# Hidden-state differences of product m6 made by VectorE instead of GpSimd, and residual reloads placed later in the load queue

## The chip, the cores and the metric

One NeuronCore of a Trainium2 chip. The metric is the device time of one launch in microseconds, the median of three runs. TensorE is called PE, VectorE DVE, ScalarE ACT, GpSimd POOL, and SyncE, whose queue issues all loads here, SP.

## The reference

A one-layer encoder trunk on 1024 tokens (two groups of 512) with width 1024. Attention and a recurrent mixer come first; the part that matters here is the second half of the layer:

```python
x = x + rmsnorm(mix, norm_mix_post[i])
h = rmsnorm(x, norm_mlp_pre[i])
m = jnp.square(jax.nn.relu(h @ w_up[i])) @ w_down[i]     # (1024 x 1024) @ (1024 x 4096), then (1024 x 4096) @ (4096 x 1024)
x = x + rmsnorm(m, norm_mlp_post[i])
e = p[i] @ w_ple[i]
gate = jax.nn.sigmoid(x @ w_ple_gate[i])
x = x + rmsnorm(e * gate, norm_ple[i])
```

All data are float32.

## The kernel before

**The work around the change.** The product with `w_down` is done by Strassen's scheme: instead of eight products of half-sized blocks there are seven, m1 to m7, each of a sum or difference of blocks of the hidden state (the operand) with a sum, difference or plain block of `w_down` (the weight). They are executed in the order of the list `products`: m4, m7, m1, m3, m5, m2, m6. Each product has 16 steps k over the contraction; a step is called a tile below, so the stage has 112 tiles. A tile is 12 matmuls of 128x512: four groups of 128 token rows, with three passes each (high x high, low x high, high x low), because every float32 number is split into a rounded high part and a rest.

**What each tile needs.** ACT makes the high parts (`wy_high` of the weight, L1392; `op_high` of the operand, L1423). POOL makes the low part of the weight, `wy_low` (L1449), and for every second tile of m7, m1 and m6 the weight's sum (`w_sum`, L1459). DVE makes the low part of the operand, `op_low` (L2194), the operand's sum where there is one (`op_sum`, L2187), the remaining weight sums (`w_sum`, L2171), and adds finished products to the result (`add_out`, L2212). All of them work up to two or three tiles ahead of PE: there are three buffers each for `wy_high`/`wy_low` (PAIRS) and for `op_high`/`op_low` (APAIRS). In the program's loops `low(pool, n + 2)`, `operand_sum(n + 3)`, `operand_low(n + 2)` stand for what is made while PE does tile n.

**The operand of m6** is the difference hid21 - hid11, one 128x512 tile for each k. These 16 differences are made ahead of m6, in place, by `hidden_difference`: eight during m5, six during m2 (four of them k = 10 to 13, then k = 0 and 1), and two (k = 14, 15) at the first tiles of m6. The table `difference_after` says behind which tile each is made. Before the change POOL makes them (L1478), right after the `wy_low` of that tile; since POOL runs two tiles ahead, the one behind tile n falls into PE's tile n - 2.

**The operand of m2** is a sum that was kept in DRAM (`keep_e`) for its first 14 tiles; SP loads it back tile by tile, beside the weight, in a ring of six buffers.

**Between m2 and m6.** When m5 is done, the first half of the result is complete. During m2, ACT squares it (`squares8`), DVE makes the mean (`means8`, behind tile 6), POOL the reciprocal root (`roots_of`, L2044, at its tile 7), and DVE does `add8(t)` for t = 0 to 3 behind tiles 8, 10, 12, 14 of m2: a 128x1024 product with the gain (L2223) and the addition to the residual `x_res` (L2227). For that the residual must be back from DRAM: SP reloads it (`x_res<-keep_x`, L1872, 512 KB for each t), t = 0 to 3 behind loads of m2, and t = 4 to 7, which `add8` needs only after m6, behind loads of m6. The first of each four waits for an addition that frees the space: that of m5 (`add_out("m5", 3, "12")`), which DVE does at tile 3 of m2, and that of m2 (`add_out("m2", 3, "22")`) at tile 7 of m6. The addition of t = 0 waits for all four reloads of its half. PE transposes the new residual at tiles 5, 8, 10 and 12 of m6 (L1566).

Each engine works off its own instructions in the order written; the engines wait for each other by counters.

Of the kernel before, what the change touches and what calls it, by code (L numbers as in the profile page):

```python
# [54 lines left out]
def trunk_kernel(nc, x, p, norm_mix_pre, w_in, w_uq, w_ukv, att_out_norm, hg_lb, hg_out_norm,  # L55
                 w_o, norm_mix_post, norm_mlp_pre, w_up, w_down, norm_mlp_post, w_ple, w_ple_gate, norm_ple,
                 rope_cos, rope_sin, latent_gain, y):
    with ExitStack() as top:
# [983 lines left out]
        def back_of():  # L1042
# [6 lines left out]
            minus = ("m4", "m3")  # L1049
            segs = [("wo", 0, h, n) for h in range(2) for n in range(2)]  # L1050
# [57 lines left out]
            def pool_sums(n):  # L1108

                if n >= TILES:  # L1110
                    return False
                (kind, _, _, _), k = segs[tiles_of[n][0]], tiles_of[n][1]
                if kind == "st":
                    return st_order[k] in ("t2", "t4")
                return kind == "m" and products[segs[tiles_of[n][0]][1]] in ("m7", "m1", "m6") and k % 2 == 1
# [4 lines left out]
            raws, splits = [], []  # L1120
            for n in range(TILES):
# [12 lines left out]
                splits.append(("pair", n))  # L1134
                if n in difference_after:
                    splits.append(("difference", difference_after[n]))
                for r in res_after.get(n, []):
                    raws.append(("res", r))
                    splits.append(("res", r))
            raw_at = {tile: q for q, tile in enumerate(raws)}  # L1140
            place = {tile: q for q, tile in enumerate(splits)}
            high_at = {tile: q for q, tile in enumerate(tile for tile in splits if tile[0] in ("pair", "res"))}
# [4 lines left out]
            a_sum_at = {n: i for i, n in enumerate(a_sums)}  # L1147
# [144 lines left out]
            def score_slices(part):  # L1292

                kind, one, two = part
                if kind == "q":
# [29 lines left out]
             hid21_in, hid_summed, sums_kept, w_sum_made, op_sum_made, op_high_made, op_low_made, out_act, out_dve) = (  # L1325
                 sem(top, "st_" + n) for n in (
                     "x_moved", "s_step", "s_split", "s_high", "t_made", "p1_made", "first_added", "first", "u", "comb", "late", "hid11_in",
                     "hid21_in", "hid_summed", "sums_kept", "w_sum", "op_sum", "op_high", "op_low", "out_act", "out_dve"))
# [29 lines left out]
            def sum_tile(n):  # L1358

                s, k = tiles_of[n]  # L1360
                return t_sum[int(st_order[k][1])][:, :] if segs[s][0] == "st" else w_sum[(n - M_TILE) % 2]

# [44 lines left out]
            def op_high_of(act, n):  # L1407
# [5 lines left out]
                elif name == "m6":  # L1413
                    act.wait_ge(low_made, place["difference", k] + 1)
                elif name == "m2" and k < SUMMED:
                    raw_ready(act, ("e", n))
                else:
                    act.wait_ge(op_sum_made, a_sum_at[n] + 1)
# [32 lines left out]
            def weight_sum(pool, n):  # L1451
                s, k = tiles_of[n]
                if segs[s][0] == "m":
# [3 lines left out]
                    if sum_before(n) is not None:  # L1457
                        pool.wait_ge(low_made, place["pair", sum_before(n)] + 1)
# [14 lines left out]
            def hidden_difference(pool, k):  # L1473
                pool.wait_ge(hid11_in, 16 * len(SPILLS))
                pool.wait_ge(hid21_in, 16 * BLOCKS)
                if k >= SUMMED:
                    pool.wait_ge(op_sum_made, a_sum_at[first[M2] + k] + 1)
                pool.tensor_tensor(hid21[k], hid21[k], hid11[k], ALU.subtract).then_inc(low_made, 1)  # L1478

            def low(pool, n):  # L1480
                if n < TILES:
                    if pool_sums(n + 1):
                        weight_sum(pool, n + 1)
                    low_part(pool, ("pair", n))
                    if n in difference_after:
                        hidden_difference(pool, difference_after[n])
# [283 lines left out]
            def sp_tail(sp):  # L1770
# [9 lines left out]
                def freed(raw):  # L1780
                    name, n = raw
                    if name in ("pair", "res"):
# [9 lines left out]
                    elif raw_of(("pair", n)) is not None:  # L1792
                        sp.wait_ge(low_made, place["pair", n] + 1)
# [28 lines left out]
                back_after = {m_raw("m2", 7 + i): i for i in range(4)}  # L1822
                back_after.update({m_raw("m6", 11 + i): 4 + i for i in range(4)})
                for q in range(len(raws)):
# [26 lines left out]
                    if q in hid11_after:  # L1851
                        b = hid11_after[q]
                        if b == SPILLS[0]:
                            sp.wait_ge(late_made, 6 * BLOCKS)
                            sp.wait_ge(low_made, place["pair", M_TILE - 1] + 1)
# [17 lines left out]
                    if q == m_raw("m2", 2):  # L1873
                        sp.wait_ge(low_made, place["difference", 3] + 1)
                        sp.wait_ge(op_sum_made, a_sum_at[first[M5] + 15] + 1)
# [189 lines left out]
            def dve_tail(dve):  # L2065
# [92 lines left out]
                def down_weight_sum(n):  # L2158
# [10 lines left out]
                    elif sum_before(n) is not None:  # L2169
                        dve.wait_ge(low_made, place["pair", sum_before(n)] + 1)  # L2170
# [3 lines left out]
                def operand_sum(n):  # L2174
                    if n not in a_sum_at:
# [444 lines left out]
```

## Time and profile before

| | |
|---|---|
| median of 3 runs | 1431.26 us (1430.6 to 1433.81) |
| profiled execution, its own time | 1430.18 us |
| its span | 1428.6 us |
| mean granted PE clock | 0.994 |
| PE busy | 1388.5 us, 97% of the span |
| PE weight loads busy | 1146.0 us, 80% |
| DVE busy | 912.4 us, 64% |
| POOL busy | 810.8 us, 57% |
| ACT busy | 659.4 us, 46% |

A busy time counts an instruction from its start to its end, and also what it waits in between for a port. The span is that from the first to the last instruction; the time of the execution has 1.6 us around it.

### The profile page before, as it was taken

The page shows a single profiled execution, that of the slowest core. Times are in us where ns is not written, and L with a number is a line of the kernel's source. Part 1 is how long each engine was busy: PE and PEld are TensorE (multiplying, and loading weights), DVE is VectorE, ACT ScalarE, POOL GpSimd, SP SyncE. Part 2 cuts the span into 40 slices and gives each one's busy share as a digit, 9 for nine tenths or more (in the row PEclk, how much of TensorE's full clock was granted, in tenths as well). Part 3 has the DMA queues.
Part 4 walks back from the last instruction along what each step waited for, and adds up shares of the span by engine and source line. Part 5 has one row for each costly group of instructions (what it writes and reads, how often), then busy time and mean ns, then how long its engine had stood idle before and what let it go on. Part 6 is the DMA issues. An engine that isn't in the chain of part 4 may idle for free.

```text
span 1428.6 us, 19101 instructions
## 1 busy us (share of the span) xinstructions
PE 1388.5 (97%) x6868; PEld 1146.0 (80%) x6868; DVE 912.4 (64%) x1096; ACT 659.4 (46%) x1225; POOL 810.8 (57%) x612
## 2 busy tenths in 40 slices
PE   7999999999999999999999999999999999889998
PEld 5888888878848999887888888888766878768876
DVE  6135555436587877165665556558999898785375
ACT  6223222324337765355765554545443444335452
POOL 4374636356306433455577777765777477765481
PEclk9999999999999999999999999999999999999999
DMA  6221011102240003434543443438466724655252
GB/s 206 67 67 38 23 39 29 31 26 60 67 102 2 1 1 104 170 104 140 185 125 104 125 125 97 132 109 296 163 198 212 252 89 151 218 164 176 89 165 86
DMA packets 138253, 162.08 MB, mean 113 GB/s; under 512 B 16688, under 2 KB 82224, under 8 KB 138160
## 3 DMA queue, kind: packets, MB, share of 16 engines
q1 hardware_dynamic: 138160, 160.87, 35.7%
q8 instruction: 55, 0.90, 0.2%
q14 instruction: 38, 0.31, 0.1%
HBM read 139.86 MB, written 18.87 MB: 111 GB/s over the span
## 4 chain that ended last, share of the span: by engine, by line
PE 80%; DVE 12%; issue 3%; POOL 2%; DMA 1%; ACT 1%; SPq 0%; DVEq 0%; POOLq 0%; ACTq 0%
PE ps L50 21%; PE ps L52 21%; PE ps L51 21%; DVE op_low L2194 4%; PE ps L921 4%; PE ps L1757 4%; DVE op_sum L2187 3%; DVE w_sum L2171 2%; PE ps L1764 2%; PE ps L1566 1%; PE ps L1014 1%; POOL wy_low L1449 1%; PE ps L968 1%; PE ps L953 1%; DMA w_raw<-keep_e 1%
## 5 line engine op out<-in xcount | busy, mean ns | idle before, releaser
L1449 POOL TENSOR_TENSOR wy_low<-w_raw,wy_high 128x512 fp32r<-128x512 f32 x118 | 176.2, 1495 | 120.7 <-ACT wy_high L1392 120.5
L50 PE MATMUL ps<-wy_high,op_high 128*128 128x512 f32 x448 | 180.0, 402 | 15.3 <-DVE op_low L2194 15.1
L51 PE MATMUL ps<-wy_low,op_high 128*128 128x512 f32 x448 | 176.1, 393 | 0.0
L52 PE MATMUL ps<-wy_high,op_low 128*128 128x512 f32 x448 | 176.1, 393 | 0.0
L1449 POOL TENSOR_TENSOR wy_low<-w_sum,wy_high 128x512 fp32r<-128x512 f32 x80 | 121.3, 1523 | 76.0 <-ACT wy_high L1392 75.9
L369 POOL TENSOR_TENSOR wx_low<-w_raw,wx_high 128x512 fp32r<-128x512 f32 (+1 forms) x64 | 84.2, 1321 | 140.4 <-ACT wx_high L471 140.4
L1392 ACT ACTIVATE wy_high<-w_raw 128x512 fp32r<-128x512 f32 x118 | 74.3, 630 | 153.6 <-PE ps L52 147.5
L50 PEld LDWEIGHTS ps<-wy_high,op_high 128*128 128x128 f32 x448 | 85.2, 190 | 45.4 <-POOL wy_low L1449 16.3
L1449 POOL TENSOR_TENSOR wy_low<-t_sum,wy_high 128x512 fp32r<-128x512 f32 x64 | 89.5, 1398 | 53.8 <-ACT wy_high L1392 53.8
L1392 ACT ACTIVATE wy_high<-w_sum 128x512 fp32r<-128x512 f32 x80 | 50.6, 632 | 126.0 <-PE ps L52 67.5
L50 PE MATMUL ps<-h_high,wx_high 128*128 128x512 f32 (+1 forms) x256 | 102.6, 401 | 0.0
L50 PE MATMUL ps<-a_high,wy_high 128*128 128x512 f32 x256 | 100.1, 391 | 0.8 <-DVE hid L2111 0.8
L52 PEld LDWEIGHTS ps<-wy_high,op_low 128*128 128x128 f32 x448 | 85.1, 190 | 18.4
L52 PE MATMUL ps<-h_high,wx_low 128*128 128x512 f32 (+1 forms) x256 | 99.8, 390 | 0.0
L51 PE MATMUL ps<-h_low,wx_high 128*128 128x512 f32 (+1 forms) x256 | 99.8, 390 | 0.0
L52 PE MATMUL ps<-a_high,wy_low 128*128 128x512 f32 x256 | 99.6, 389 | 0.0
L51 PE MATMUL ps<-a_low,wy_high 128*128 128x512 f32 x256 | 99.6, 389 | 0.0
L51 PEld LDWEIGHTS ps<-wy_low,op_high 128*128 128x128 f32 x448 | 85.3, 190 | 16.5
L515 ACT ACTIVATE k_pick<-kk 128x512 f32<-128x512 f32 x56 | 35.9, 669 | 114.3 <-DVE kk L688 108.0
L50 PE MATMUL ps<-wy_high,a_high 128*128 128x512 f32 x224 | 88.6, 396 | 0.0
L685 DVE TENSOR_TENSOR qq<-qq,totals 128x512 f32<-128x512 f32 x48 | 41.3, 861 | 72.3 <-PE ps L921 72.3
L52 PE MATMUL ps<-wy_high,a_low 128*128 128x512 f32 x224 | 87.4, 390 | 0.0
(270 smaller groups left out, 3658.8 us busy)
## 6 DMA issues: line engine op xcount, KB each, us to landing
w_raw<-in_w_down SPq DMA_DIRECT2D x127, 256.0 KB, 3.4
raw_more<-in_w_down SPq DMA_DIRECT2D x65, 256.0 KB, 3.4
w_raw<-in_w_up SPq DMA_DIRECT2D x64, 256.0 KB, 3.3
w_raw<-in_w_in SPq DMA_DIRECT2D x62, 256.0 KB, 2.8
w_raw<-in_w_o SPq DMA_DIRECT2D x32, 256.0 KB, 2.6
raw_more<-in_w_up SPq DMA_DIRECT2D x32, 256.0 KB, 3.3
w_raw<-in_w_ple_gate SPq DMA_DIRECT2D x32, 256.0 KB, 2.6
keep_h<-comb SPq DMA_DIRECT2D x26, 256.0 KB, 2.3
```

Of the source, the lines that this page charges most:

```text
L50: pe.matmul(out, stat_high, mov_high, start=start, stop=False)
L51: pe.matmul(out, stat_high, mov_low, start=False, stop=False)
L52: return pe.matmul(out, stat_low, mov_high, start=False, stop=stop)
L369: pool.tensor_tensor(out, raw, high.bitcast(F32), ALU.subtract).then_inc(w_low_made, 1)
L515: act.activation(k_pick[:, g, l % 2, :].rearrange("p (b h t) -> p b h t", h=2, t=1 << l), halves(kk, g, l, False), ACT.Copy).then_inc(k_pi ...
L685: dve.tensor_tensor(queries, queries, factors(g, l, True), ALU.mult).then_inc(q_decayed, 1)
L921: last = pe.matmul(ps[:, 4 + g, ch * P:(ch + 1) * P], k_pick[:, g, l % 2, ch * P:(ch + 1) * P], halves(qq, g, l, True, ch, 1), start=True, ...
L1392: act.activation(out, tile_raw(tile), ACT.Copy).then_inc(high_made, 1)
L1449: pool.tensor_tensor(low_tile, tile_raw(tile), high_tile.bitcast(F32), ALU.subtract).then_inc(low_made, 1)
L1757: last = pe.matmul(ps[:, 4 + tr % 2, hr * VD:(hr + 1) * VD], prob_t[:, r % 2, k, :], v_att[:, tr // QT * QT + k, hr * VD:(hr + 1) * VD], s ...
L2187: dve.tensor_tensor(op_sum[n % 2], one[k], two[k], ALU.subtract if name == "m7" else ALU.add).then_inc(op_sum_made, 1)
L2194: dve.tensor_tensor(op_low[n % APAIRS][:, :], op_raw(n), op_high[n % APAIRS][:, :].bitcast(F32), ALU.subtract).then_inc(op_low_made, 1)
```

## The change

Three things change.

1. The differences go from POOL to DVE. `low` on POOL no longer makes them; DVE's loop calls `hidden_difference(difference_after[n])` at tile n, behind `operand_low(n + 2)`. The table stays the same, so each is also made two tiles later than before in PE's terms. They count on the counter of operand sums (`op_sum_made`), and whoever waited for them waits there.
2. The reloads of the residual for t = 0 to 3 stand behind the loads of tiles 9 to 12 of m2 instead of 7 to 10; those for t = 4 to 7 stand behind the last load of m6 and the three loads after it (of the gate product) instead of behind tiles 11 to 14 of m6.
3. Code that would let DVE make the low parts of some weights is added, with an empty list `low_on_dve`, so it issues nothing.

```diff
@@ the tables
+            low_on_dve = ()
...
-                splits.append(("pair", n))
-                if n in difference_after:
-                    splits.append(("difference", difference_after[n]))
+                highs.append(("pair", n))
+                if not low_by_dve(n):
+                    splits.append(("pair", n))
...
-            a_sum_at = {n: i for i, n in enumerate(a_sums)}
+            a_made = []
+            for n in range(M_TILE, M_TILE + MSTEPS + 3):
+                a_made += [("sum", n)] if n in a_sums else []
+                a_made += [("difference", difference_after[n - 3])] if n - 3 in difference_after else []
+            made_at = {made: i for i, made in enumerate(a_made)}
@@ ACT: op_high_of
                 elif name == "m6":
-                    act.wait_ge(low_made, place["difference", k] + 1)
+                    act.wait_ge(op_sum_made, made_at["difference", k] + 1)
@@ POOL
-            def hidden_difference(pool, k):
-                pool.wait_ge(hid11_in, 16 * len(SPILLS))
-                pool.wait_ge(hid21_in, 16 * BLOCKS)
-                if k >= SUMMED:
-                    pool.wait_ge(op_sum_made, a_sum_at[first[M2] + k] + 1)
-                pool.tensor_tensor(hid21[k], hid21[k], hid11[k], ALU.subtract).then_inc(low_made, 1)
...
-                    low_part(pool, ("pair", n))
-                    if n in difference_after:
-                        hidden_difference(pool, difference_after[n])
+                    if not low_by_dve(n):
+                        low_part(pool, ("pair", n))
@@ SP
-                back_after = {m_raw("m2", 7 + i): i for i in range(4)}
-                back_after.update({m_raw("m6", 11 + i): 4 + i for i in range(4)})
+                back_after = {m_raw("m2", 9 + i): i for i in range(4)}
+                back_after.update({m_raw("m6", 15) + i: 4 + i for i in range(4)})
...
                     if q == m_raw("m6", 7):
-                        sp.wait_ge(low_made, place["difference", BLOCKS - 1] + 1)
+                        sp.wait_ge(op_sum_made, len(a_made))
@@ DVE
+                def hidden_difference(k):
+                    if k == 2:
+                        dve.wait_ge(hid21_in, 16 * BLOCKS)
+                    if k >= SUMMED:
+                        dve.wait_ge(op_sum_made, made_at["sum", first[M2] + k] + 1)
+                    dve.tensor_tensor(hid21[k], hid21[k], hid11[k], ALU.subtract).then_inc(op_sum_made, 1)
...
                     down_weight_sum(n + 3)
                     operand_sum(n + 3)
                     operand_low(n + 2)
+                    weight_low(n + 2)
+                    if n in difference_after:
+                        hidden_difference(difference_after[n])
```

**DVE, from behind tile 7 of m2 to behind tile 11.** The first pair L2223, L2227 (before) or L2247, L2251 (after) is `add8(0)`. Before:

```order
L2194 TENSOR_TENSOR op_low0_219<-w_raw,op_high0_216 128x512
L2223 SCALAR_TENSOR_TENSOR total_116<-total_116,y_stat12_134,gain_mlp_244 128x1024
L2227 TENSOR_TENSOR x_res_119<-x_res_119,total_116 128x1024
L2194 TENSOR_TENSOR op_low1_220<-w_raw,op_high1_217 128x512
L2194 TENSOR_TENSOR op_low2_221<-raw_more1_159,op_high2_218 128x512
L2223 SCALAR_TENSOR_TENSOR total_116<-total_116,y_stat12_134,gain_mlp_244 128x1024
L2227 TENSOR_TENSOR x_res_119<-x_res_119,total_116 128x1024
L2187 TENSOR_TENSOR op_sum0_222<-hid21_14_214,p1_kept_160 128x512
L2194 TENSOR_TENSOR op_low0_219<-w_raw,op_high0_216 128x512
```

After:

```order
L2205 TENSOR_TENSOR op_low0_219<-w_raw,op_high0_216 128x512
L2247 SCALAR_TENSOR_TENSOR total_116<-total_116,y_stat12_134,gain_mlp_244 128x1024
L2251 TENSOR_TENSOR x_res_119<-x_res_119,total_116 128x1024
L2205 TENSOR_TENSOR op_low1_220<-w_raw,op_high1_217 128x512
L2219 TENSOR_TENSOR hid21_0_200<-hid21_0_200,hid11_0_166 128x512
L2205 TENSOR_TENSOR op_low2_221<-raw_more1_159,op_high2_218 128x512
L2247 SCALAR_TENSOR_TENSOR total_116<-total_116,y_stat12_134,gain_mlp_244 128x1024
L2251 TENSOR_TENSOR x_res_119<-x_res_119,total_116 128x1024
L2198 TENSOR_TENSOR op_sum0_222<-hid21_14_214,p1_kept_160 128x512
L2205 TENSOR_TENSOR op_low0_219<-w_raw,op_high0_216 128x512
L2219 TENSOR_TENSOR hid21_1_201<-hid21_1_201,hid11_1_167 128x512
```

Two subtractions into hid21, for k = 0 and k = 1, stand between the low parts and the additions.

**POOL at the same place**, around the reciprocal root of the first half (`y_stat12<-y_stat11`). Before:

```order
L1478 TENSOR_TENSOR hid21_13_213<-hid21_13_213,hid11_13_179 128x512
L1449 TENSOR_TENSOR wy_low_120<-w_raw,wy_high_121 128x512
L1449 TENSOR_TENSOR wy_low_120<-raw_more0_158,wy_high_121 128x512
L1478 TENSOR_TENSOR hid21_0_200<-hid21_0_200,hid11_0_166 128x512
L2044 TENSOR_TENSOR y_stat12_134<-y_stat11_133,minus_half 128x4
L1449 TENSOR_TENSOR wy_low_120<-w_raw,wy_high_121 128x512 x2
L1478 TENSOR_TENSOR hid21_1_201<-hid21_1_201,hid11_1_167 128x512
L1449 TENSOR_TENSOR wy_low_120<-raw_more0_158,wy_high_121 128x512
L1449 TENSOR_TENSOR wy_low_120<-w_raw,wy_high_121 128x512 x3
L1459 TENSOR_TENSOR w_sum1_225<-w_raw 128x512
```

After:

```order
L1466 TENSOR_TENSOR wy_low_120<-w_raw,wy_high_121 128x512 x2
L1466 TENSOR_TENSOR wy_low_120<-raw_more0_158,wy_high_121 128x512
L2055 TENSOR_TENSOR y_stat12_134<-y_stat11_133,minus_half 128x4
L1466 TENSOR_TENSOR wy_low_120<-w_raw,wy_high_121 128x512 x2
L1466 TENSOR_TENSOR wy_low_120<-raw_more0_158,wy_high_121 128x512
L1466 TENSOR_TENSOR wy_low_120<-w_raw,wy_high_121 128x512 x3
L1476 TENSOR_TENSOR w_sum1_225<-w_raw 128x512
```

The three differences of this piece (one further up, one right ahead of the root, one between the low parts behind it) are gone; the low parts of the weights and the weight's sum keep their order.

**SP's queue in m2**, from the load of tile 7's weight on. `w_raw` and `raw_more` are the ring of six buffers. Before:

```order
L1778 DMA w_raw<-in_w_down 128x512
L1872 DMA x_res_119<-keep_x 128x1024
L1778 DMA w_raw<-keep_e 128x512
L1778 DMA w_raw<-in_w_down 128x512
L1872 DMA x_res_119<-keep_x 128x1024
L1778 DMA w_raw<-keep_e 128x512
L1778 DMA raw_more0_158<-in_w_down 128x512
L1872 DMA x_res_119<-keep_x 128x1024
L1778 DMA raw_more1_159<-keep_e 128x512
L1778 DMA w_raw<-in_w_down 128x512
L1872 DMA x_res_119<-keep_x 128x1024
```

After:

```order
L1787 DMA w_raw<-in_w_down 128x512
L1787 DMA w_raw<-keep_e 128x512
L1787 DMA w_raw<-in_w_down 128x512
L1787 DMA w_raw<-keep_e 128x512
L1787 DMA raw_more0_158<-in_w_down 128x512
L1883 DMA x_res_119<-keep_x 128x1024
L1787 DMA raw_more1_159<-keep_e 128x512
L1787 DMA w_raw<-in_w_down 128x512
L1883 DMA x_res_119<-keep_x 128x1024
L1787 DMA w_raw<-keep_e 128x512
L1787 DMA w_raw<-in_w_down 128x512
L1883 DMA x_res_119<-keep_x 128x1024
L1787 DMA w_raw<-keep_e 128x512
L1787 DMA raw_more0_158<-in_w_down 128x512
L1883 DMA x_res_119<-keep_x 128x1024
```

Four loads of m2 (the kept operands of tiles 7 and 8, the weights of tiles 8 and 9) now stand ahead of the first reload.

## Rows read from the trace of the kernel before

**Rows 1.** PE busy by stretch: window in us, its length, busy us (matmuls), clock, DMA share, GB/s
```profile
1109.56:1153.08 43.52, 43.52 (x193) 1.00 0.66 208
1153.08:1198.22 45.14, 44.34 (x194) 1.00 0.34 109
1198.22:1248.21 49.99, 46.00 (x193) 0.97 0.61 205
1248.21:1305.49 57.28, 50.87 (x225) 0.94 0.58 195
```

**Rows 2.** timeline of PE: start us, duration us, what, [idle before it <-releaser]
```profile
1219.98 0.46 PE L50 MATMUL ps<-wy_high,op_high 128*128 128x512 f32 x1
...
1231.89 0.76 PE L50 MATMUL ps<-wy_high,op_high 128*128 128x512 f32 x1 [3.10 <-DVE op_low L2194]
...
1255.16 0.47 PE L50 MATMUL ps<-wy_high,op_high 128*128 128x512 f32 x1 [4.07 <-DVE op_low L2194]
...
1279.33 1.68 PE L1566 MATMUL ps<-ident,x_res 128*128 128x128 f32 x8 [2.35 <-DVE total L2212]
```

**Rows 3.** PE busy and clock in the stretches behind the first two waits
```profile
1231.80:1235.20 3.40, 3.31 (x8) 0.50 0.61 179
...
1255.10:1259.30 4.20, 4.14 (x11) 0.59 0.65 215
```

**Rows 4.** timeline of all engines in one tile of m3
```profile
1147.64 0.39 PE L50 MATMUL ps<-wy_high,op_high 128*128 128x512 f32 x1
1147.77 0.69 DVE L2187 TENSOR_TENSOR op_sum<-hid,hid 128x512 f32<-128x512 f32 x1
...
1148.61 1.30 POOL L1449 TENSOR_TENSOR wy_low<-w_raw,wy_high 128x512 fp32r<-128x512 f32 x1 [1.42 <-ACT wy_high L1392]
...
1149.09 1.37 DVE L2194 TENSOR_TENSOR op_low<-op_sum,op_high 128x512 fp32r<-128x512 f32 x1 [0.63 <-ACT op_high L1423]
```

**Rows 5.** timeline of DVE in m5
```profile
1168.36 1.67 DVE L2187 TENSOR_TENSOR op_sum<-hid,hid 128x512 f32<-128x512 f32 x1
1169.95 1.78 DVE L2194 TENSOR_TENSOR op_low<-op_sum,op_high 128x512 fp32r<-128x512 f32 x1
1171.76 1.67 DVE L2187 TENSOR_TENSOR op_sum<-hid,hid 128x512 f32<-128x512 f32 x1
```

**Rows 6.** timeline of POOL in m5
```profile
1169.44 1.74 POOL L1478 TENSOR_TENSOR hid<-hid,hid 128x512 f32<-128x512 f32 x1
```

**Rows 7.** timeline of DVE in the second half of m2
```profile
1224.41 1.20 DVE L2194 TENSOR_TENSOR op_low<-w_raw,op_high 128x512 fp32r<-128x512 f32 x1 [1.48 <-ACT op_high L1423]
1225.53 2.31 DVE L2223 SCALAR_TENSOR_TENSOR total<-total,y_stat,gain_mlp 128x1024 f32<-128x1024 f32 x1
1227.88 2.19 DVE L2227 TENSOR_TENSOR x_res<-x_res,total 128x1024 f32<-128x1024 f32 x1
1230.00 1.75 DVE L2194 TENSOR_TENSOR op_low<-w_raw,op_high 128x512 fp32r<-128x512 f32 x1
...
1233.34 1.27 DVE L2223 SCALAR_TENSOR_TENSOR total<-total,y_stat,gain_mlp 128x1024 f32<-128x1024 f32 x1
1234.65 1.22 DVE L2227 TENSOR_TENSOR x_res<-x_res,total 128x1024 f32<-128x1024 f32 x1
```

**Rows 8.** timeline of POOL there
```profile
1222.33 1.46 POOL L2044 TENSOR_TENSOR y_stat<-y_stat,minus_half 128x4 f32<-128x4 f32 x1
...
1226.73 2.26 POOL L1478 TENSOR_TENSOR hid<-hid,hid 128x512 f32<-128x512 f32 x1
```

**Rows 9.** waits of SP's queue from 1195 to 1310 us: total us, times, longest
```profile
SPq L1872 <- DVE total L2212: 12.8, 2, 8.9
```

**Rows 10.** waits of ACT from 1210 to 1230 us: total us, times, longest
```profile
ACT op_high L1423 <- DMA w_raw<-keep_e: 2.9, 2, 1.6
...
ACT op_high L1423 <- DMA raw_more<-keep_e: 1.3, 1, 1.3
```

**Rows 11.** issues of the first and the fourth reload (1210.3 to 1210.7, 1214.6 to 1215): KB, us to landing
```profile
x_res<-keep_x SPq DMA_DIRECT2D x1, 512.0 KB, 3.6
...
x_res<-keep_x SPq DMA_DIRECT2D x1, 512.0 KB, 8.4
```

**Rows 12.** groups of instructions from 1153 to 1305 us: count, busy us, mean ns, idle before
```profile
L2212 DVE TENSOR_TENSOR total<-part,ps 128x512 f32<-128x512 f32 x16 | 10.5, 674 | 0.0
```

More of the change, by code:

```diff
@@ L1114, in pool_sums, with low_by_dve @@
                     return st_order[k] in ("t2", "t4")
-                return kind == "m" and products[segs[tiles_of[n][0]][1]] in ("m7", "m1", "m6") and k % 2 == 1
+                return kind == "m" and products[segs[tiles_of[n][0]][1]] in ("m7", "m1", "m6") and k % 2 == 1 and not low_by_dve(n)
+            def low_by_dve(n):
+                return in_m(n) and m_step(n)[0] in low_on_dve
             difference_after = {first[M5] + 2 * i + 1: 2 + i for i in range(8)}
@@ L1139, in back_of @@
                     splits.append(("res", r))
+                    highs.append(("res", r))
             raw_at = {tile: q for q, tile in enumerate(raws)}
             place = {tile: q for q, tile in enumerate(splits)}
-            high_at = {tile: q for q, tile in enumerate(tile for tile in splits if tile[0] in ("pair", "res"))}
+            high_at = {tile: q for q, tile in enumerate(highs)}
+            low_at = {n: i for i, n in enumerate(n for n in range(TILES) if low_by_dve(n))}
             w_sums = [n for n in range(M_TILE, M_TILE + MSTEPS) if len(quads[m_step(n)[0]]) == 2 and not pool_sums(n)]
@@ L1361, in sum_tile, with low_ready @@
                 return t_sum[int(st_order[k][1])][:, :] if segs[s][0] == "st" else w_sum[(n - M_TILE) % 2]
+            def low_ready(engine, n):
+                if low_by_dve(n):
+                    engine.wait_ge(w_low_made, low_at[n] + 1)
+                else:
+                    engine.wait_ge(low_made, place["pair", n] + 1)
             def sum_before(n):
@@ L1457, in weight_sum @@
                     if sum_before(n) is not None:
-                        pool.wait_ge(low_made, place["pair", sum_before(n)] + 1)
+                        low_ready(pool, sum_before(n))
                     pool.tensor_tensor(sum_tile(n), raw_tile(one), raw_tile(two),
@@ L1792, in freed @@
                     elif raw_of(("pair", n)) is not None:
-                        sp.wait_ge(low_made, place["pair", n] + 1)
+                        low_ready(sp, n)
                     else:
@@ L1854, in sp_tail @@
                             sp.wait_ge(late_made, 6 * BLOCKS)
-                            sp.wait_ge(low_made, place["pair", M_TILE - 1] + 1)
+                            low_ready(sp, M_TILE - 1)
                             for i in range(4):
@@ L2169, in down_weight_sum @@
                     elif sum_before(n) is not None:
-                        dve.wait_ge(low_made, place["pair", sum_before(n)] + 1)
+                        low_ready(dve, sum_before(n))
                     dve.tensor_tensor(sum_tile(n), raw_tile(one), raw_tile(two),
@@ L2524, in pe_tail @@
                     n, last_k, width = first[a] + b, depth[segs[a][0]] - 1, len(banks_of(a))
-                    pe.wait_ge(low_made, place["pair", n] + 1)
+                    low_ready(pe, n)
                     wh, wl = wy_high[:, n % PAIRS, :], wy_low[:, n % PAIRS, :]
```

23 lines of the change are left out of this document (15 added, 8 removed).

## The prediction

> **What bounds the kernel now.** I read first how long PE takes for each product, from the view of busy time by stretch [rows 1]. m3 takes 43.52 us for 16 tiles without a gap: 2.72 us a tile, PE's own pace. m5 takes 45.14 us, 1.6 more. m2 takes 49.99, 6.5 more. m6 takes 57.28, of which four transposes of eight matmuls each are work (about 0.8 us each, 3.3 together), so it loses some 10.5. Only these losses can be won: the products before m5 hold nothing that the change touches, and behind m6 only the place of the reloads differs.
>
> Next, where PE stands, from its timeline [rows 2]. It waits 3.10 us for the low operand of tile 11 of m2 (until 1231.89), 4.07 us for that of tile 1 of m6 (until 1255.16), and 2.35 us at the second transpose of m6 for an addition by DVE. Behind each wait the clock is at the lower of its two levels, 1.2 GHz, for about 3.4 us [rows 3]: 3.40 us at 0.50, so about 1.7 us of PE's work is lost on top of the wait. I call T8 the start of tile 8 of m2, 1219.98 [rows 2]; from there to 1255.16, where tile 1 of m6 starts, nine tiles take 35.2 us instead of 24.5.
>
> So DVE is late in m2. Why, the timelines of DVE and POOL tell. Where they don't meet, DVE needs 0.69 us for a 128x512 tile from two SBUF operands, and POOL 1.30 [rows 4]. The DVE instruction that starts while POOL's runs takes 1.37, and ends 0.55 us after POOL's end (1149.91 to 1150.46). In m5 POOL makes differences too [rows 6], the two alternate, and each DVE instruction takes 1.67 to 1.78, starts 1.6 to 1.8 apart [rows 5]: 0.6 of work and 1.1 behind one of POOL's. An addition that reads PSUM takes 0.67 on the mean over the same stretch [rows 12] and seems never to wait. So count turns: a DVE instruction 0.6, a POOL instruction that gets ahead of it 1.1.
>
> **Differences in m5 (eight).** Now a pair of tiles in m5 has on DVE 2 operand sums and 2 low parts (4 x 0.6), on POOL 3 instructions (3 x 1.1): 5.7 us of turns in 5.44 us of PE. That is over PE's pace, and the rows show tiles of 3.4 us, DVE-bound. After: 5 x 0.6 + 2 x 1.1 = 5.2 us, below it. The additions of m3 in tiles 0 to 3 (0.6 each, no turn) lie beside POOL's turns. In the steady tile of m3, POOL starts 0.97 us after the tile's start and DVE's low part ends 2.82 us after it (1147.64 to 1150.46) [rows 4]; it is needed two tiles on, at 5.44, so 2.6 us are spare, more than a difference costs even in its worst turn (1.75). I take **-1.6 us** for m5, all its loss. Bounds: 0 if every DVE instruction still meets POOL, -1.6 at best.
>
> The Trainium skill speaks against this step (the page SBUF — State Buffer, section "SBUF: two separate sides"): the port pair that VectorE and GpSimd share is an exclusive lock, held for the whole instruction, and the loser stands still. The rows agree that the loser stands still. With the whole 1.30 us of POOL's instruction as its turn, a pair of tiles would hold 2 x 1.3 + 5 x 0.6 = 5.6 us, over 5.44, and m5 would lose 8 x 0.16 = 1.3 us as it does now, so the step would bring 0.3 instead of 1.6.
>
> **Reloads in m2.** The first reload waits for DVE's addition at tile 3. SP stands there 12.8 - 8.9 = 3.9 us [rows 9], and behind it the kept operands and weights of tiles 7 to 9. Then four times 512 KB go out among them, and ACT waits 2.9 + 1.3 us for kept operands [rows 10]. The low part of tile 10 thus starts at 1224.41, ends at 1225.6, and `add8(0)` follows [rows 7]. After the change the first reload is queued behind tile 9's weight, which itself needs a buffer that tile 6's low weight frees; by then the addition of tile 3 is done, so SP doesn't stand, and a tile of 2.72 us carries 1 MB. The operands come in time. The low part of tile 10 is then done at the steady place, T8 + 2.8 (1222.8), 2.8 us earlier. The root, at 1222.33 to 1223.79 now [rows 8], moves up too: its input no longer waits for late operands and no difference is ahead of it.
>
> The reload of t = 3 goes out with tile 12's weight, about T8 - 0.2. Landing took 3.6 us for the first and 8.4 for the fourth of the present burst [rows 11]; spread out, I take 5, so T8 + 4.8, and the addition of `add8(0)` wants it at T8 + 5.2. Tight; late by 3 us at the upper bound.
>
> **m2 from tile 8 on.** Here the count goes along DVE's order, with 0.6 for a 512-wide instruction, 1.3 and 1.2 for the two halves of `add8` (the last two of [rows 7]), and 1.1 for each POOL instruction that has become ready. In us behind T8: low part of tile 10 done 2.8; `add8(0)` first half 4.1; POOL 5.2; second half 6.4; low part of tile 11 **7.0** (PE wants it at 8.2: the 3.10 us wait is gone); POOL and difference 0 until 8.7; low part of tile 12 9.3 (wanted 10.9); POOL, half, half of `add8(1)` 13.0; POOL, operand sum 14.7; POOL 15.8; low part of tile 13 **16.4**, wanted at 13.6. So a wait comes back two tiles later: 2.8 us, and the clock falls, 1.7. Then difference 1 17.0, sum and low part of tile 14 18.2, `add8(2)` 20.7, POOL's weight sum 21.8, weight sum and low part of tile 15 23.0 (in time), low part of m6 tile 0 24.8, `add8(3)` with two POOL turns 29.5, weight sum and low part of m6 tile 1 **30.7**, wanted at 29.0. PE starts that tile at 30.8 instead of 35.2: **-4.4 us**. The differences 0 and 1 cost 1.2 us in this chain; what they replace is POOL's four differences in it (0, 1, 14, 15), of which each stood before a DVE instruction: 2.19, 2.31 and 1.75 us in a row [rows 7] for 1.2, 1.3 and 0.6. The second bound: if the freed turns bring nothing, the chain is only 2.8 us earlier and 1.2 longer, -1.6. At best the wait at tile 13 doesn't come, and -9 stands.
>
> The wait ahead of m6 tile 1 shrinks from 4.07 to about 1.8 us. The clock fell behind waits of 2.35 and more [rows 2, 3]; in m5, which loses 1.6 us in short waits, it stays at 1.00 [rows 1]. I take it that it stays up: **-1.7 us**; 0 is the other bound.
>
> **Start of m6.** Differences 14 and 15 are now DVE's, at tiles 0 and 1, beside additions, low parts and a weight sum: 1.2 us in a place where DVE is behind, at worst 2 x 1.75 = 3.5. Whatever is not made up until tile 7 lengthens PE's wait for the last addition there (2.35 us [rows 2]), since DVE comes to it in order. I take **+1.2 us**.
>
> **Reloads in m6.** SP stands 8.9 us [rows 9] before the reload of t = 4 and holds the loads of tiles 12 and 13 back. PE doesn't wait for these: m6's loss of 10.5 is used up by its two waits [rows 2] and 1.7 of clock behind each, so tiles 8 to 15 are at pace. After, they come early and the reloads go with the gate's first weights, 2 MB and 1 MB, wanted after m6. 0, covered by m6's last four tiles (11 us); uncovered, it would show as a wait of gate tile 1 or 2. The load of `gain_ple`, which waited for POOL's difference 15, now waits for DVE's, some 1 to 3 us, with two weights behind it that are wanted a tile or two later: 0.
>
> **Sum.** -1.6 - 4.4 - 1.7 + 1.2 = -6.5 us against the profiled execution: 1430.18 - 6.5 = 1423.7, span about 1422.1. That execution is 1.1 below the median, so the median to expect is 1431.26 - 6.5 = **1424.8**.
>
> **Rivals.** (a) *No wait comes back at tile 13.* POOL and DVE fall in step so that DVE meets fewer of its instructions. For it: in one row pair `add8(1)` runs free (1.27, 1.22). Against: it ran free because PE stood and POOL had no work. Gain 1.6 + 9 + 0 to 1.7: about 1420. Chance 0.15. (b) *Half the gain:* the clock falls ahead of m6 as well and DVE's backlog is carried to the second transpose in full, +2.7 instead of +1.2: -1.6 - 4.4 + 2.7 = -3.3, 1428. For it: DVE's gaps in m6 between tiles 1 and 7 are small. Chance 0.2. (c) *The reloads are late.* All four must have landed for `add8(0)`; with 8.4 us they land 3 us late, the low part of tile 11 at T8 + 10: -3.5, 1427.8. It decides above 5 us of landing. Chance 0.1. (d) *Slower:* the four differences on the late DVE cost a full turn each, 4 x 1.75 = 7.0, because POOL, ahead with less to do, is always ready when DVE ends; only m5's 1.6 and the 2.8 of the operands stand against it: +2.6, 1433.9. It decides when POOL meets more than two of three DVE instructions from T8 on. Against: POOL has 4 instructions fewer there. Chance 0.07. (e) *Nothing:* DVE's total of work is longer by 16 x 0.6 us and the gain in m5 and m2 is given back in m6, so only a shift of the waits is left: 1431, 0.06. My forecast has the rest, 0.42.
>
> **Numbers.** A run of this kernel can be told from no change beyond about 0.2%, 2.9 us: below 1428.4 is faster. My own case (1422 to 1427) and (a) count wholly as faster, (b) and (c) by about two thirds: 0.42 + 0.15 + 0.2 = 0.77. Slower is (d), 0.07. The rest, 0.16, is the same. The range leaves out half of (a) below and (d) and part of (e) above: 1419.5 to 1430.5.
>
> **What the changed profile would show.** m5 at 43.5 us; no L2219 longer than 1.8; no wait of SP's reload for DVE and no wait of ACT for `keep_e`; tile 11 of m2 without a wait, one of 2 to 3 us at tile 13 with half clock behind it; m6 tile 1 at most 2 us late and at full clock; the wait at m6's second transpose at 2 to 5 us. Wrong would be: the second half of `add8(0)` waiting for a DMA, or DVE's instructions behind tile 8 as long as now.

## The result, and the profile after

| | before | changed |
|---|---|---|
| median of the runs timed together | 1432.53 us (6 runs, 1430.6 to 1434.12) | 1424.24 us (6 runs, 1422.3 to 1427.27) |
| profiled execution: its time, span | 1430.18, 1428.6 us | 1422.3, 1420.5 us |
| mean granted PE clock | 0.994 | 0.997 |
| DVE busy, POOL busy | 912.4, 810.8 us | 907.0, 780.1 us |

The ratio is 0.9945, 95% interval 0.9929 to 0.9961: 8 us faster, with 5.6 to 10 in the interval. The forecast was 6.5.

Busy time of PE by stretch, m3, m5, m2, m6 as in [rows 1], and then the rest of the span, in the changed kernel:

```profile
1110.28:1153.80 43.52, 43.52 (x194) 1.00 0.66 207
1153.80:1197.32 43.52, 43.52 (x194) 1.00 0.37 114
1197.32:1245.43 48.11, 44.49 (x193) 1.00 0.63 211
1245.43:1298.68 53.25, 48.10 (x225) 1.00 0.63 210
1298.68:1420.50 121.82, 114.67 (x529) 0.98 0.34 110
```

m5 is at PE's own pace, m2 is 1.9 us shorter and m6 4.0. (Behind m6 it is 121.8 us instead of 123.1; m5 starts 0.7 us later.) The clock is 1.00 from m3 to m6; before the change it fell in m2 (0.97) and m6 (0.94). That is not wholly the change's doing, as a second profile of the same kernel showed (below, `changed_again`).

PE's timeline, as in [rows 2], with T8 first and then every wait up to tile 1 of m6:

```profile
1219.08 0.39 PE L50 MATMUL ps<-wy_high,op_high 128*128 128x512 f32 x1
...
1227.97 0.47 PE L50 MATMUL ps<-wy_high,op_high 128*128 128x512 f32 x1 [0.57 <-DVE op_low L2205]
1235.02 0.47 PE L50 MATMUL ps<-wy_high,op_high 128*128 128x512 f32 x1 [1.36 <-DVE op_low L2205]
1242.63 0.47 PE L50 MATMUL ps<-wy_high,op_high 128*128 128x512 f32 x1 [1.69 <-DVE op_low L2205]
1250.26 0.47 PE L50 MATMUL ps<-wy_high,op_high 128*128 128x512 f32 x1 [1.95 <-DVE op_low L2205]
```

In place of waits of 3.10, 0.77 and 4.07 us, at tiles 11 and 15 of m2 and tile 1 of m6, there are four of 0.57 to 1.95 us, at tiles 11, 13 and 15 of m2 and tile 1 of m6. From T8 to the last of them it is 31.2 us instead of 35.2. SP's queue no longer waits for DVE's additions [rows 9]; its new wait, that of the load of `gain_ple` for difference 15, is short:

```profile
SPq L1891 <- DVE hid L2219: 0.3, 1, 0.3
```

ACT waits for no kept operand [rows 10]. But DVE now waits for the reload, 1.82 us ahead of the second half of `add8(0)`; the prediction had named this wait as a sign of being wrong (timeline of DVE, which answers to [rows 7]):

```profile
1220.52 1.36 DVE L2205 TENSOR_TENSOR op_low<-w_raw,op_high 128x512 fp32r<-128x512 f32 x1 [0.76 <-ACT op_high L1440]
1221.80 1.27 DVE L2247 SCALAR_TENSOR_TENSOR total<-total,y_stat,gain_mlp 128x1024 f32<-128x1024 f32 x1
1224.90 1.23 DVE L2251 TENSOR_TENSOR x_res<-x_res,total 128x1024 f32<-128x1024 f32 x1 [1.82 <-DMA x_res<-keep_x]
1226.04 1.78 DVE L2205 TENSOR_TENSOR op_low<-w_raw,op_high 128x512 fp32r<-128x512 f32 x1
1227.74 0.68 DVE L2219 TENSOR_TENSOR hid<-hid,hid 128x512 f32<-128x512 f32 x1
```

The fourth reload was issued at 1219.02, 0.06 us ahead of T8, and took longer to land than the 5 us that I had taken (issues from 1219.0 to 1219.4):

```profile
x_res<-keep_x SPq DMA_DIRECT2D x1, 512.0 KB, 5.8
```

### The profile page after: what moved, and what is told of

Same layout as the page of the kernel before. It is cut to its first block, busy times and chain, and to the rows that moved or that the text cites. A ratio compares the mean times of both kernels' runs of the same rounds, so it can differ in the third digit from the quotient of the medians.

```text
span 1420.5 us, 19085 instructions
## 1 busy us (share of the span) xinstructions
PE 1381.4 (97%) x6868; PEld 1141.4 (80%) x6868; DVE 907.0 (64%) x1112; ACT 657.6 (46%) x1225; POOL 780.1 (55%) x596
## 4 chain that ended last, share of the span: by engine, by line
PE 82%; DVE 11%; issue 3%; DMA 1%; POOL 1%; ACT 1%; SPq 0%; DVEq 0%; POOLq 0%; ACTq 0%
PE ps L50 22%; PE ps L52 22%; PE ps L51 22%; PE ps L921 4%; PE ps L1766 4%; DVE op_low L2205 3%; DVE op_sum L2198 2%; DVE w_sum L2182 2%; PE ps L1773 2%; PE ps L1575 1%; PE ps L1014 1%; PE ps L968 1%; PE ps L953 1%; PE ps L965 1%; DMA k_t<-k_rope 0%
## 5 line engine op out<-in xcount | busy, mean ns | idle before, releaser
L51 PE MATMUL ps<-wy_low,a_high 128*128 128x512 f32 x224 | 87.2, 389 | 0.0
```

The lines of the kernel that those rows point to most:

```text
L51: pe.matmul(out, stat_high, mov_low, start=False, stop=False)
```

## The experiments

All were timed in five rounds beside the kernel before. Ratios are to that kernel. Where I compare with the changed kernel, I use the lengths of the stages in the profiles (one profiled execution for each run), which repeat to 0.1 us where nothing is late, while single runs of one kernel lie up to 7 us apart.

### Each half of the change alone

`differences_alone`: the reloads back.

```diff
-                back_after = {m_raw("m2", 9 + i): i for i in range(4)}
-                back_after.update({m_raw("m6", 15) + i: 4 + i for i in range(4)})
+                back_after = {m_raw("m2", 7 + i): i for i in range(4)}
+                back_after.update({m_raw("m6", 11 + i): 4 + i for i in range(4)})
```

> The changed kernel with both groups of reloads at their old places, so the differences are DVE's and nothing else differs from before. Theory A (each part has its own share: fewer port turns for DVE, and operands that come in time): m5 falls from 45.1 to 43.5 us; in m2 SP still stands about 4 us before the first reload and ACT still waits about 4 us for kept operands, so add8(0) starts as late as before, but with fewer turns behind it; in all 3 to 5 us faster than before, ratio 0.997. Theory B (the reloads' place does it, the differences win only in m5): 1.6 us faster, 0.999, and tile 11 of m2 waits 3 us as before. Theory C (the differences do it all): 8 us faster, 0.9945.

`reloads_alone`: the kernel before with the two new lines.

> The kernel before with both groups of reloads at their new places; the differences stay on POOL. Theory A: m5 stays at 45.1 us; kept operands come in time, the low part of tile 10 is done 2 to 3 us earlier, but POOL's difference stands ahead of the root and the turns of POOL stay, so m2 and m6 together lose 2 to 3 us less: 2 to 3 us faster, ratio 0.998. Theory B: 6 us faster, 0.996. Theory C: no change, 1.000.

Both medians are 1429.03 us, both ratios 0.997 (0.9959 to 0.9982, and 0.9957 to 0.9983). Each half gives 0.3%, together they give 0.55%: theory A. B and C fall by `differences_alone`, whose interval holds neither the 0.999 of B nor the 0.9945 of C; `reloads_alone` alone would not tell A (0.998) from B (0.996), but it excludes C (1.000). The stages m5, m2, m6 of `differences_alone`:

```profile
1157.24:1200.76 43.52, 43.52 (x193) 1.00 0.36 115
1200.76:1251.90 51.14, 44.73 (x193) 1.00 0.59 199
1251.90:1307.05 55.15, 50.84 (x225) 0.94 0.59 202
```

and of `reloads_alone`:

```profile
1154.17:1199.30 45.13, 44.36 (x193) 1.00 0.34 109
1199.30:1247.20 47.90, 44.33 (x194) 1.00 0.63 212
1247.20:1305.64 58.44, 52.03 (x226) 0.91 0.56 192
```

The differences win m5 (43.52) and the start of m6; with the old reloads m2 is even longer than before (51.14 against 49.99), with waits at tiles 8, 11, 13 and 15. The reloads' place wins m2 (47.90), but m6 still waits 4.07 us for its tile 1, as before, and at a clock of 0.91 instead of 0.94 takes 1.2 us longer. In `differences_alone` SP stands before its reloads, and ACT waits even longer than before for kept operands (waits of SP from 1195 to 1310 us, of ACT from 1195 to 1250):

```profile
SPq L1883 <- DVE total L2236: 12.5, 2, 7.8
...
ACT op_high L1440 <- DMA w_raw<-keep_e: 6.4, 3, 2.6
```

### Where the gain in m5 comes from

`m5_on_pool`: differences 2 to 9 back on POOL, the others on DVE.

```diff
+            on_pool = tuple(range(2, 10))
...
+                    if difference_after.get(n) in on_pool:
+                        k = difference_after[n]
+                        pool.wait_ge(hid11_in, 16 * len(SPILLS))
+                        pool.wait_ge(hid21_in, 16 * BLOCKS)
+                        pool.tensor_tensor(hid21[k], hid21[k], hid11[k], ALU.subtract).then_inc(low_made, 1)
...
-                    if n in difference_after:
+                    if n in difference_after and difference_after[n] not in on_pool:
                         hidden_difference(difference_after[n])
```

> The changed kernel with the eight differences of m5 back on POOL; the other eight stay on DVE. Theory A (turns: 5.7 us a pair of tiles against 5.2): m5 is back at 45.1 us with low parts and sums of 1.7 us, m2 and m6 as in the changed kernel (48.1 and 53.2 us): 1.6 us slower than the changed kernel. Rival (the lock is held for POOL's whole instruction, so m5 is bound either way, or the m5 gain came from elsewhere): m5 stays within 0.3 us of 43.5.

`all_in_m5`: fourteen differences behind tiles 1 to 14 of m5.

```diff
-            difference_after = {first[M5] + 2 * i + 1: 2 + i for i in range(8)}
-            difference_after.update({first[M2] + 2 * i + 1: (10 + i) if i < 4 else i - 4 for i in range(6)})
+            difference_after = {first[M5] + 1 + i: (2 + i) if i < 12 else i - 12 for i in range(14)}
```

> The changed kernel with the fourteen differences 2 to 13, 0 and 1 behind tiles 1 to 14 of m5, one each, none in m2. Theory A (turns: 6 x 0.6 + 2 x 1.1 = 5.8 us for a pair of tiles against PE's 5.44): m5 becomes DVE-bound in its second half, 45 to 46 us instead of 43.5; m2 has two differences fewer where DVE is late, 1.2 us less: in all 0 to 1.5 us slower than the changed kernel. Rival 1 (turns cost DVE more, a full 1.7 for each instruction): m5 over 50 us. Rival 2 (a difference costs DVE only its 0.6 where POOL is idle, 4 x 0.6 + 2 x 0.6 + 1.3 = 4.9 a pair): m5 stays at 43.5 us.

`m5_on_pool`: 1425.15 us, ratio 0.9947 (0.9931 to 0.9963). `all_in_m5`: 1424.83 us, 0.9944 (0.993 to 0.9957). In time neither is told apart from the changed kernel; in m5 they are (busy time of PE in m5, first `m5_on_pool`):

```profile
1153.55:1198.66 45.11, 44.34 (x194) 1.00 0.34 109
```

and `all_in_m5`, m5 and m2:

```profile
1155.37:1200.06 44.69, 44.53 (x193) 1.00 0.36 110
1200.06:1246.10 46.04, 44.09 (x193) 1.00 0.66 222
```

With the differences back on POOL the 1.6 us are back. With one on DVE for every tile m5 is 1.2 us over PE's pace, where rival 2 wanted none and rival 1 a stage of over 50. I had written 45 to 46 us and got 44.69: tiles 0 to 8 take 2.72 us, since DVE enters the stage ahead, and only tiles 9 to 13 take 2.91 to 3.04. In those tiles the turns can be read one by one (timeline of DVE and POOL in `all_in_m5`):

```profile
1186.70 1.32 POOL L1465 TENSOR_TENSOR wy_low<-w_raw,wy_high 128x512 fp32r<-128x512 f32 x1 [1.59 <-ACT wy_high L1408]
1186.78 1.79 DVE L2204 TENSOR_TENSOR op_low<-op_sum,op_high 128x512 fp32r<-128x512 f32 x1
1188.49 0.68 DVE L2218 TENSOR_TENSOR hid<-hid,hid 128x512 f32<-128x512 f32 x1
1189.09 0.68 DVE L2197 TENSOR_TENSOR op_sum<-hid,hid 128x512 f32<-128x512 f32 x1
1189.69 1.78 DVE L2204 TENSOR_TENSOR op_low<-op_sum,op_high 128x512 fp32r<-128x512 f32 x1
```

DVE's instructions start 1.71, 0.60 and 0.60 us apart: 2.91 us a tile, 5.8 a pair, which is the count of 6 x 0.6 + 2 x 1.1. The one that meets POOL's ends 0.55 us behind POOL's end, as in [rows 4]. So the count tells whether DVE binds: at 5.7 and 5.8 us a pair m5 is longer than PE's 43.5 us, at 5.2 it isn't. It doesn't tell how long the stage becomes: 5.8 gave 44.69 and 5.7 gave 45.11. DVE's lead counts as well (tiles 0 to 8 at pace); what else makes this difference was not tested. The rule of the Trainium skill (the page SBUF — State Buffer, section "SBUF: two separate sides"), taken with the whole 1.3 us for POOL, asked for 1.3 us of loss in the changed m5. The profile has none; the measurement decides for 1.1. That the loser stands still is what all these rows show.

The groups of instructions from 1154 to 1197 us, a stretch that lies within m5 in both kernels, of `m5_on_pool`: mean ns of one ahead of the second bar:

```profile
L2217 DVE TENSOR_TENSOR op_low<-op_sum,op_high 128x512 fp32r<-128x512 f32 x14 | 20.3, 1453 | 0.1
L2210 DVE TENSOR_TENSOR op_sum<-hid,hid 128x512 f32<-128x512 f32 x13 | 18.1, 1391 | 0.3
```

and of the changed kernel:

```profile
L2205 DVE TENSOR_TENSOR op_low<-op_sum,op_high 128x512 fp32r<-128x512 f32 x14 | 17.9, 1281 | 1.9 <-ACT op_high L1440 1.8
L2198 DVE TENSOR_TENSOR op_sum<-hid,hid 128x512 f32<-128x512 f32 x13 | 13.3, 1022 | 0.2
L2219 DVE TENSOR_TENSOR hid<-hid,hid 128x512 f32<-128x512 f32 x7 | 4.7, 678 | 0.0
```

Without POOL's differences an operand sum takes 1.02 us on the mean instead of 1.39, a low part 1.28 instead of 1.45, and the differences themselves 0.68. DVE makes the eight differences as well, and yet its busy time in m5 falls, from 42.4 us in `m5_on_pool` to 39.3 in the changed kernel.

### What each difference costs where DVE is late

`early_0_1`: differences 0 and 1 behind tiles 4 and 6 of m2 instead of 9 and 11.

```diff
-            difference_after.update({first[M2] + 2 * i + 1: (10 + i) if i < 4 else i - 4 for i in range(6)})
+            difference_after.update({first[M2] + 2 * i + 1: 10 + i for i in range(4)})
+            difference_after.update({first[M2] + 4: 0, first[M2] + 6: 1})
```

> The changed kernel with the differences 0 and 1 made behind tiles 4 and 6 of m2, where DVE stands idle 1.3 us a tile, instead of behind 9 and 11. Theory A (each costs the late DVE 0.6 us, up to 1.7 with a turn): the chain up to m6 tile 1 is 1.2 us shorter, m2 and the first tiles of m6 together 1.2 us less; 1 us faster. Rival (the port turns bind, not DVE's own work): below 0.3 us.

1422.79 us, ratio 0.9925 (0.9911 to 0.9939): the lowest median here. m2 takes 46.01 us, 2.1 less than in the changed kernel's first profile and 1.65 less than in its second, against 1.2 expected. What is over 1.2 is not the two instructions' doing: the fourth reload landed after 4.4 us in this execution, and after 5.8 and 5.3 in those two. `m6_reloads_back` (below) has the m2 of the changed kernel and ends `add8(0)` 6.2 us behind T8, as this run does, and its m2 takes 47.22 us: 1.2 more, as expected. `all_in_m5` has the same 46.04 in m2, which shows it a second time.

`early_and_later` does this and moves differences 14 and 15 from behind tiles 0 and 1 of m6 to tiles 2 and 3.

```diff
-            difference_after.update({first[M6] + i: 14 + i for i in range(2)})
+            difference_after.update({first[M6] + 2 + i: 14 + i for i in range(2)})
```

> Differences 0 and 1 behind tiles 4 and 6 of m2, and 14 and 15 behind tiles 2 and 3 of m6 instead of 0 and 1. Theory A (each of them costs the late DVE 0.6 to 1.7 us at the start of m6): the waits at tiles 2 and 4 of m6 (0.3 and 0.8 us) shrink or move, since DVE catches up only towards tile 7: the same as with the early differences alone, up to 0.5 us, ratio 0.9925. Rival (they cost their full turn and nothing takes it back): 1 us faster.

1426.68 us, 0.9959 (0.9946 to 0.9971): both theories wrong, it is slower than `early_0_1`. m2 is the same (46.04), m6 56.73 us instead of 53.22. The waits tell why: of SP's queue from 1195 to 1310 us, of DVE and of PE from 1244 to 1300:

```profile
SPq L1892 <- DVE hid L2220: 7.1, 1, 7.1
...
DVE w_sum L2183 <- DMA w_raw<-in_w_down: 3.6, 1, 3.6
...
PE ps L1576 <- DVE total L2237: 5.4, 2, 4.3
```

The load of `gain_ple` overwrites operands of the differences, so it waits for the last of them, now 7.1 us. Behind it in the queue are weights of m6; DVE waits 3.6 us for one, and its additions, which stand behind that sum, hold up PE's second transpose for 4.3 us instead of 2.3. Behind that longer wait the clock falls, where in `early_0_1` it stays up: PE is busy 49.4 us in m6 instead of 48.1, so 1.3 of the 3.5 us are the clock's. Two tiles of delay of a 0.6 us instruction cost 3.5 us by way of the queue. I had named this wait in the prediction for the changed kernel and priced it at nothing, which was right there (0.3 us).

### The reloads' place, finer

`m2_reloads_8`: the changed kernel with `m_raw("m2", 8 + i)` instead of `9 + i`.

> The changed kernel with the first four reloads one tile earlier, behind the loads of tiles 8 to 11 of m2. Theory A (add8(0) waits 1.82 us for the fourth reload, and everything behind it is late by that): the wait goes, tile 11 starts without one, the chain of DVE up to m6 tile 1 ends 1 to 2 us earlier: 1 to 2 us faster than the changed kernel, unless the operands of tiles 9 and 10 come late. Rival (DVE's turns with POOL bind, the wait only lets POOL go first): the same up to 0.5 us, since the waits at tiles 13 and 15 take it back.

`early_and_8`: the same on top of `early_0_1`.

> Differences 0 and 1 behind tiles 4 and 6 of m2, and the first four reloads behind tiles 8 to 11. Theory A (the earlier reload meets DVE's addition again, SP stands 2 us and the kept operand of tile 8 comes late, which costs as much as the wait at add8(0)): m2 0 to 1 us longer than with the early differences alone (46.0 us). Rival (only the wait at add8(0) counts): m2 0.5 us shorter.

1425.54 us, 0.9944 (0.993 to 0.9957), and 1423.33 us, 0.9928 (0.9915 to 0.9941). The wait of `add8(0)` for the reload is gone in both, and nothing is won: m2 takes 48.58 us in the first (46.66 in the second, 0.65 longer than with the early differences alone). SP stands again 2.0 us for DVE's addition at tile 3, and ACT waits 4.2 us in all for kept operands (waits of SP, then of ACT, in `m2_reloads_8`):

```profile
SPq L1883 <- DVE total L2236: 2.0, 1, 2.0
...
ACT op_high L1440 <- DMA w_raw<-keep_e: 2.6, 2, 1.3
ACT op_high L1440 <- DMA raw_more<-keep_e: 1.6, 1, 1.6
```

So one tile earlier is too early: DVE doesn't wait at `add8(0)`, but comes to it later. The wait that the place of the change brings is 1.82 us in its first profile, with other lengths in others, since the same reload took 4.9 to 5.8 us to land. DVE gets some 1.0 us of it back: while it stands, POOL's instruction gets through, and the second half of `add8(0)` then takes 1.23 us, where it takes 2.21 in `m2_reloads_8`. What counts is when `add8(0)` is done:

| | DVE's wait for the reload | `add8(0)` done behind T8 | m2 |
|---|---|---|---|
| `m6_reloads_back` | 0.89 us | 6.2 us | 47.22 us |
| `changed_again` | 1.36 | 6.6 | 47.66 |
| `m5_on_pool` | 1.48 | 6.7 | 47.79 |
| changed kernel | 1.82 | 7.1 | 48.11 |
| `m2_reloads_8` | none | 7.4 | 48.58 |
| `early_0_1` | 0.48 | 6.2 | 46.01 |
| `early_and_8` | none | 6.8 | 46.66 |

Within the first five, and again within the last two, m2 follows that time nearly one for one; between the groups lie 1.2 us, the two differences. The wait for the reload thus cost the changed kernel 0.9 us in its first profile, and nothing in `m6_reloads_back`.

`m6_reloads_back`: only the second group of reloads at its old place.

> The changed kernel with only the second four reloads at their old place behind tiles 11 to 14 of m6. Theory A (covered by the last tiles of m6): SP stands about 9 us again before the reload of t = 4, loads of tiles 12 and 13 come late, PE doesn't wait for them; m6 and the rest stay at 53.2 and 121.9 us within 0.5, time within 0.1% of the changed kernel. Rival (this part of the change brought the shorter stage behind m6, 123.1 to 121.9 us, or some of m6's gain): 1 to 3 us slower than the changed kernel.

1426.09 us, 0.9948 (0.9932 to 0.9965): the same as the changed kernel. SP stands 7.8 us before the reload again, m6 takes 55.52 us and what follows it, up to PE's last matmul, 115.26, near the second profile of the changed kernel (55.14 and 115.57). Tiles 13 and 14 of m6 take 3.01 and 2.85 us here instead of 2.72: POOL waits 4.4 us for the weight of a late load, and PE for POOL's low part. So this half of the reloads' move is worth about 0.4 us in the profile, too little to be seen in the times.

### The order on DVE behind tile 11 of m2

`low_first`: low part ahead of the sums.

```diff
-                    down_weight_sum(n + 3)
-                    operand_sum(n + 3)
-                    operand_low(n + 2)
+                    if first[M2] + 11 <= n < first[M2] + 16:
+                        operand_low(n + 2)
+                        down_weight_sum(n + 3)
+                        operand_sum(n + 3)
+                    else:
+                        down_weight_sum(n + 3)
+                        operand_sum(n + 3)
+                        operand_low(n + 2)
```

> The changed kernel with DVE making the low part of tile n + 2 ahead of the sums of tile n + 3, from behind tile 11 of m2 to behind tile 15. Nothing is left out, only the order on DVE. Theory A (PE waits at tiles 13, 15 and m6 tile 1 for a low part that stands behind a sum wanted a tile later): these three waits shrink by 0.6 to 1.7 us each, 1 to 3 us faster. Rival (the sums are then late by as much, DVE's total binds): the waits move to the next tile, the same up to 0.5 us.

1424.73 us, 0.9946 (0.9932 to 0.9959). The rival is right: PE waits 0.76 us at tile 13 instead of 1.36, but 2.08 at tile 15 instead of 1.69, with the clock falling there, 0.93 at m6 tile 1 and 1.02 at tile 3. From T8 to tile 1 of m6 it is 31.3 us, against 31.2 in the changed kernel: DVE has too much to do there, in this order as in that.

### The same kernel once more

> The changed kernel unaltered, to be compared with the next two on one chip and to see where the clock falls in another execution. Theory A (the waits are set by the order of instructions, the falls of the clock by where a wait happens to lie): the stages from m4 to m2 repeat to 0.1 us (43.6, 49.9, 49.6, 43.5, 43.5; m2 between 47.2 and 48.2), waits at the same tiles, and m6 is 53.2 us without a fall or about 55 with two. Rival (the full clock in m6 is owed to the change): m6 is 53.2 us again, clock 1.00 from m4 to m6.

1426.7 us, ratio 0.9952 (0.9939 to 0.9965). m5 43.52, m2 47.66, m6 55.14 us. PE waits 1.28, 1.71 and 1.94 us at tiles 13 and 15 of m2 and tile 1 of m6, nearly as before (1.36, 1.69, 1.95); at tile 11 only about 0.2 instead of 0.57, since the reload landed earlier. But here the clock falls behind the wait at m6 tile 1 and again behind the second transpose. The stretch of 3.4 us from half a microsecond behind the wait's end, here

```profile
1254.30:1257.70 3.40, 3.40 (x10) 0.50 0.84 290
```

and, from the wait's end, in the first profile:

```profile
1250.30:1253.70 3.40, 3.40 (x15) 1.00 0.82 255
```

## Why the prediction was right

The time, 1424.24 us, is 0.6 below the 1424.8 of the forecast and within the range; against the kernel before timed beside it the gain is 8.3 us where I had 6.5, and the second series of the same kernel has 6.8 (1433.45 to 1426.7). The mechanism was right in m5 and in what freed DVE in m2; that the sum came so near is in part luck, since two of its terms hold in one execution and not in another. By steps:

- **Differences in m5, -1.6.** Right: 45.14 to 43.52, and 45.11 when they go back to POOL. The 1.3 us of loss set against this step were not worked out for the kernel before: with the whole 1.30 us as POOL's turn it would hold 3 x 1.3 + 4 x 0.6 = 6.3 us a pair and lose 8 x 0.86 = 6.9 us in m5. It lost 1.6, so the rows before already spoke against that turn.
- **The operands in time.** Right: no wait of ACT for them; the low part of tile 10 ended at T8 + 2.8 as written.
- **The reload tight, late by 3 us at the upper bound.** It landed at T8 + 5.7 instead of T8 + 4.8, and DVE stood 1.82 us. The sign of being wrong that names this wait came true, and rival (c) came in part: landing took 5.8 us, not 5. It cost 0.9 us and not its full length, as `m6_reloads_back` and `m2_reloads_8` show.
- **The chain from tile 8 on, -4.4.** Measured -4.0 (31.2 us from T8 to m6 tile 1 instead of 35.2; forecast 30.8). In three more executions with the same instructions there it is 30.3 to 30.9. Its inside was less right: I had one wait of 2.8 us at tile 13 with the clock falling behind it, and there are waits of 0.57, 1.36 and 1.69 us at tiles 11, 13 and 15 with no fall in this execution. The low part of tile 11 came at T8 + 8.7, not 7.0, by the reload. What was right is that DVE is bound there and a wait comes back two tiles on.
- **The clock ahead of m6, -1.7.** Tile 1 of m6 took 2.85 us instead of 4.41, so -1.6 in the profiled execution, but I had argued it from the wait's length, and that fails: after the same wait it fell in `changed_again`. The size is right for one execution, and over several only a part of it is the change's.
- **Start of m6, +1.2.** Tiles 2 to 6 of m6 take 15.9 us instead of 14.5, +1.3, with new waits of 0.26 us at tile 3 and 0.59 at the first transpose. They weren't carried to the second transpose, where PE still waits 2.34 us. In `changed_again`, where PE was slowed by the clock, this term is nothing (14.6 us).
- **Reloads in m6, 0.** Right to 0.4 us, by `m6_reloads_back`.

The forecast sum is 6.5 and the span lost 8.1. What stands against the 1.6 us between them: at the second transpose the clock didn't fall either (tile 8 took 2.85 us, before 3.95), and the stretch behind m6 is 1.3 us shorter, of which the change has no part that a run shows: up to PE's last matmul it takes 114.67 us here and 115.57 in the second execution of the same kernel. From the start of m5 to PE's last matmul the first profile gains 8.8 us on the kernel before, and the second 6.5, the number of the forecast, but by other terms: 1.6 in m5, 4.5 in the chain and 0.4 behind m6, with nothing from the clock ahead of m6 and nothing lost at m6's start.

Rival (d), slower by POOL meeting every difference, falls: of the sixteen differences on DVE fifteen took 0.68 us and one 1.77. Rival (a) did not come: PE waits at tile 13 in every run with the differences on DVE, 0.62 us (`early_and_8`) at the least. Of rival (b) one half came in `changed_again`, the fall of the clock ahead of m6; the other did not, since the wait at the second transpose is 2.35 us there as before.

## What to carry to other kernels

Where two engines share a port, count the turns of both per unit of work, not their busy times: moving an instruction from the one that holds the port for 1.1 us to the one that needs it for 0.6 freed 0.5 us a pair of tiles, and made the receiver's other instructions shorter as well (an operand sum 1.02 us on the mean instead of 1.39). Such a count tells whether the receiver binds, not how long the stage will be. Then place what was moved where the receiver is idle: the same two instructions, five tiles earlier, brought another 1.2 us. A transfer that waits for space should stand in its queue behind the point where the space is free, and whatever it overwrites must be done by then, or everything queued behind it pays.

## What the runs showed of the hardware that I had not expected

The clock fell behind a wait of 1.94 us in one execution, and not behind one of 1.95 in another of the same kernel. Ten of the profiles have a wait of 1.93 to 1.95 us ahead of m6 tile 1; behind it the clock fell in six and not in four. A fall costs 1.2 to 1.6 us there (the tile takes 4.02 to 4.43 us against 2.82 to 2.85). Two or three falls that come or go would be most of the 5 us between the single runs of the changed kernel; where the clock fell is known for the profiled executions only, but the mean granted clock is known for all: the fastest run of the changed kernel had 0.997 (1422.3 us) and the slowest of the same series 0.993 (1427.27 us). Over the 77 runs of the changed kernel and the variants above, each taken against the mean of its kernel, time and clock have a correlation of -0.70. So about half of the scatter (0.70 squared) goes with the clock; what makes the rest was not shown.

The same 512 KB reload, issued at the same point of the same stream of loads, took 4.9 to 5.8 us to land in four executions (`m6_reloads_back` 4.9, `changed_again` 5.3, `m5_on_pool` 5.4, the changed kernel 5.8). That moved m2 by 0.9 us between executions of the same instructions.
